# Gates spread by DMA, forgetting attention set up inside the input projection, and a delta rule on unscaled keys

## The chip, the cores and the metric

The kernel runs on one core of one Trainium2 chip. The metric is the time of one execution on the device, in microseconds (us). The engines of a core are TensorE (PE in the profile; PEld is its weight load), VectorE (DVE), ScalarE (ACT), GpSimd (POOL) and SyncE (SP), beside 16 DMA engines. Each runs its own list of instructions and waits for others on semaphores.

## The reference, cut to what matters

256 tokens of 1024 channels go through two blocks. The first has two layers, each a mixer (pooling, then attention with 16 heads) and a squared-ReLU MLP; the outcome of each of these four parts is multiplied by a gate of one value per channel before it is added to `x`. The second block puts 16 learned tokens in front, projects with `w_in` (3592 columns), and runs a gated delta rule (4 heads of 128) beside a forgetting attention (8 heads of 64):

```python
def l2norm(x): ...                       # x * rsqrt(sum(x*x) + eps)
q, k, v = split(silu(causal_dwconv(qkv, conv_w)))      # q, k, v of 4 heads x 128
q = l2norm(q) * DK ** -0.5;  k = l2norm(k);  beta = sigmoid(b_raw)
g = -exp(a_log) * softplus(a_raw + dt_bias)            # gc is its running sum
# a_mat: (k beta) k^T, below the diagonal, times exp(gc_i - gc_j)
rhs = jnp.concatenate([v * beta[..., None], k * (beta * jnp.exp(gc))[..., None]], axis=-1)
sol = lax.linalg.triangular_solve(a_mat + jnp.eye(chunk), rhs, left_side=True, lower=True, unit_diagonal=True)
u, w = sol[..., :dv], sol[..., dv:]
qk = jnp.einsum("bhncd,bhnsd->bhncs", q, k) * decay
...
v_new = u_c - w_c @ state
o_c = (q_c * exp(g_c)) @ state + qk_c @ v_new
state = state * exp(g_last) + (k_c * exp(g_last - g_c))^T @ v_new
o = o * lax.rsqrt(jnp.mean(o * o, axis=-1, keepdims=True) + EPS) * norm_w * silu(z)

# forgetting attention: c = cumsum(log_sigmoid(f_raw + f_bias))
sc = einsum("bqhd,bkhd->bhqk", q, k) * scale + c_q - c_k      # causal, softmax, times v
```

Then come `w_out`, a SwiGLU network and a last norm.

## The kernel before

Tokens are held in two tiles of 128 (index `m`), the learned tokens in one of 16 beside them (`META`). Every fp32 weight is split into a high part (`wh`, ACT, L570) and a low part (`wl`, DVE, L1074); activations are split too (`H` L1055, `L` L1057), and TensorE makes three passes for a product, H·wh, H·wl and L·wh. Weights come in tiles of 2 MB, in a ring of four slots. A tile has two halves (`hb`); a half is split in two steps, and TensorE waits for both.

Nothing is scheduled by a tool. Each engine's list is written by hand, and an engine runs its list in that order, so an instruction that waits holds up all behind it.

**Gates.** The gate vector lies with one channel to a partition (`modc`), and the residual needs it as a row on all partitions. `gate_diag` (DVE, L1018) multiplies the identity by a gate column, eight times; `gate_mm` (PE, L1668) multiplies a matrix of ones by each of these; `gate_copy` (DVE, L1026) takes the two banks to the tile `gate`. This happens for MLP0 in its last tile of `w_down`, and for the output projection `w_o` and MLP1 one after the other between attention and `w_o` (PE loop `wo_out`, L1637), behind the transposes of L1608.

**Input projection.** `w_in` has seven tiles (L1945, 272 token columns to a matmul; tile 3 is token-major, L1637). Tiles 0 to 2 give q, k, v of the delta rule, which DVE convolves (L1321), tile 3 its gate z, tiles 4 to 6 those of the forgetting attention. Small products of `wsm` give beta, the decays and the forget gate; DVE and ACT make `beta`, `gdec` and `tks` of them (L1347 to L1356, L741 to L746). ACT copies the results from PSUM (L764).

**Forgetting attention.** After the last tile PE makes the running sums (L1957, L1961), ACT copies them to `ncT` and `EG` (L771, L773), PE spreads a row of the sums to all partitions for each head (L1969), DVE copies these to `cm0`/`cm1` (L1361), and POOL masks them (L486, L489). Scores (L1978, L1981), a minimum on DVE, exponentials on ACT (L789), transposes (L2006, L2008) and the product with v (L2016 to L2020) follow in a loop over the heads, two at a time.

**Delta rule.** After the loop PE transposes q, k and v to token-major (L2027), ACT and DVE take the norms (L810, L1409), DVE scales keys and queries in eight passes and two small ones (L1427 to L1431), PE transposes all of these back (L2046, L2052), copies go to SBUF (L1434, L832), and PE makes the products K·K and Q·K (L2065, L2062). DVE multiplies them by the decays (L1448), POOL masks level 0 (L532), and the inverse of the triangular system starts: transposes (L2073, L2075), then six levels of x (L2085) and z (L2095, L2096). POOL makes each level's mask and, in between, the right sides (L513 to L520). At the end stand u, w, the state and the output with its norm (L2106 to L2134, L1493 to L1499), and the transposes for `w_out` (L1608).

## Time and profile before

| | us |
|---|---|
| median of 3 executions | 1131.53 |
| lowest, highest | 1131.45, 1134.54 |
| the profiled execution | 1124.33 |
| its span, first to last instruction | 1122.6 |
| first matmul of `w_in` | 660.98 |
| the loop over the heads, its first transpose (L2006) | 769.73 |
| first z product of level 1 | 828.36 |
| first matmul of `w_out` | 889.51 |

The profiled execution took 7.2 us less than the median; all sums are made in its times. A row of the timeline gives start, duration, engine, line, operation, output and inputs with sizes, how many instructions it groups, and in brackets the idle time before it with what ended it. A product of fp32 numbers of 128 columns counts as two instructions there, a transpose as one. The clock of a stretch is the share of full speed that was granted to TensorE: 1.00 is 2.4 GHz, 0.50 is 1.2 GHz.

### The profile page before, as it was taken

Reading aid. Unit: us, or ns where it says so; the run is one execution under the profiler, and the core shown is the slowest. Engines: PE = TensorE matmul, PEld = TensorE weight load, DVE = VectorE, ACT = ScalarE, POOL = GpSimd, SP = SyncE. Lnnn points to the kernel's source line nnn. Section 1 sums busy time; section 2 is a strip of 40 time slices with the busy share of each in tenths; the row PEclk is TensorE's granted clock in tenths of the full one; section 3 lists DMA queues with packets and bytes.
Section 4 is the critical chain, followed back from the end, with each engine's and each line's share of the span. In section 5 each row is a group of like instructions: output and inputs, shape, how many; then the busy total and the mean of one; then the engine's idle time right before and its main releaser. Section 6 shows DMA issues by size and latency. Waiting matters only on the chain.

```text
span 1122.6 us, 16534 instructions
## 1 busy us (share of the span) xinstructions
PE 1012.2 (90%) x6589; PEld 894.4 (80%) x6589; DVE 637.1 (57%) x1003; ACT 461.2 (41%) x747; POOL 112.6 (10%) x106
## 2 busy tenths in 40 slices
PE   3779999998998788899999969999789789999996
PEld 1449889996996687799889869996688669999995
DVE  1466677777546975554554465624544554454454
ACT  2344444442434212544444454536321344344343
POOL 2012010121000000111111200002063000000000
PEclk8889999999899659899999979998699789999999
DMA  9997686785546662345454523550000124646620
GB/s 327 371 387 276 231 293 226 273 288 216 198 157 220 224 226 79 144 151 215 158 215 181 213 86 105 214 168 1 1 1 1 38 75 141 196 154 204 201 78 38
DMA packets 105186, 195.60 MB, mean 174 GB/s; under 512 B 2283, under 2 KB 46572, under 8 KB 105132
## 3 DMA queue, kind: packets, MB, share of 16 engines
q1 hardware_dynamic: 104380, 192.58, 48.7%
q0 software_dynamic: 752, 2.26, 0.6%
q8 instruction: 38, 0.62, 0.2%
q14 instruction: 16, 0.13, 0.0%
HBM read 193.76 MB, written 1.07 MB: 174 GB/s over the span
## 4 chain that ended last, share of the span: by engine, by line
PE 78%; DVE 12%; ACT 3%; DMA 3%; issue 2%; POOL 1%; SPq 0%; DVEq 0%; POOLq 0%; ACTq 0%
PE ps L1691 28%; PE ps L1709 15%; PE ps L1945 7%; PE ps L2154 5%; PE ps L1637 4%; PE ps L1832 4%; DMA raw<-in_w_mod 3%; DVE wl L1074 3%; DVE accu L977 2%; ACT arena L587 1%; PE ps L2085 1%; PE ps L2096 1%; POOL x L450 1%; PE ps L1859 1%; PE ps L2095 1%
## 5 line engine op out<-in xcount | busy, mean ns | idle before, releaser
L1074 DVE TENSOR_TENSOR wl<-raw,wh 128x1024 fp32r<-128x1024 f32 (+1 forms) x288 | 315.4, 1138 | 266.9 <-ACT wh L570 266.9
L570 ACT ACTIVATE wh<-raw 128x1024 fp32r<-128x1024 f32 (+1 forms) x288 | 268.4, 982 | 352.7 <-PE ps L1691 188.3
L1691 PE MATMUL ps<-H,wh 128*128 128x256 f32 x864 | 245.4, 284 | 5.8 <-DVE L L1057 4.7
L1691 PE MATMUL ps<-H,wl 128*128 128x256 f32 x864 | 245.6, 284 | 0.0
L1691 PE MATMUL ps<-L,wh 128*128 128x256 f32 x864 | 245.2, 284 | 0.0
L1691 PEld LDWEIGHTS ps<-H,wh 128*128 128x128 f32 x864 | 166.1, 192 | 9.3 <-issue 8.3
L1691 PEld LDWEIGHTS ps<-L,wh 128*128 128x128 f32 x864 | 166.3, 192 | 0.0
L1691 PEld LDWEIGHTS ps<-H,wl 128*128 128x128 f32 x864 | 165.4, 191 | 0.9
L1709 PE MATMUL ps<-wh,aTh 128*128 128x512 f32 x256 | 101.8, 398 | 1.6 <-DVE wl L1074 1.6
L1709 PE MATMUL ps<-wl,aTh 128*128 128x512 f32 x256 | 101.2, 395 | 0.0
L1709 PE MATMUL ps<-wh,aTl 128*128 128x512 f32 x256 | 101.1, 395 | 0.0
L461 POOL TENSOR_TENSOR arena<-arena 128x512 f32<-128x512 f32 x32 | 56.2, 1755 | 309.3 <-ACT arena L615 309.3
L1945 PE MATMUL ps<-H,wh 128*128 128x272 f32 x192 | 57.8, 301 | 2.0 <-DVE L L1057 1.7
L1709 PEld LDWEIGHTS ps<-wh,aTh 128*128 128x128 f32 x256 | 48.0, 188 | 12.6 <-issue 1.6
L1945 PE MATMUL ps<-L,wh 128*128 128x272 f32 x192 | 57.4, 299 | 0.0
L1709 PEld LDWEIGHTS ps<-wh,aTl 128*128 128x128 f32 x256 | 48.0, 187 | 11.8
L1945 PE MATMUL ps<-H,wl 128*128 128x272 f32 x192 | 57.3, 298 | 0.0
L1709 PEld LDWEIGHTS ps<-wl,aTh 128*128 128x128 f32 x256 | 48.0, 188 | 11.0
L1608 PE MATMUL ps<-ident,arena 128*128 128x128 f32 x128 | 22.1, 335 | 24.2 <-DVE arena L1040 19.3
L1608 PEld LDWEIGHTS ps<-ident,arena 128*128 128x128 f32 x128 | 18.7, 175 | 27.9 <-DVE arena L1040 19.6
L1945 PEld LDWEIGHTS ps<-H,wh 128*128 128x128 f32 x192 | 38.1, 198 | 2.5 <-issue 2.5
L1832 PE MATMUL ps<-H,wh 128*128 128x256 f32 x128 | 36.8, 287 | 2.1 <-DVE L L1057 2.1
(376 smaller groups left out, 1685.3 us busy)
## 6 DMA issues: line engine op xcount, KB each, us to landing
raw<-in_w_up SPq DMA_DIRECT2D x16, 2048.0 KB, 8.7
raw<-in_w_down SPq DMA_DIRECT2D x16, 2048.0 KB, 7.7
raw<-in_w_mod SPq DMA_DIRECT2D x12, 2048.0 KB, 16.1
raw<-in_w_in SPq DMA_DIRECT2D x7, 2048.0 KB, 7.6
raw<-in_w_mod SPq DMA_DIRECT2D x12, 1024.0 KB, 7.1
raw<-in_w_qkv SPq DMA_DIRECT2D x6, 2048.0 KB, 11.1
raw<-in_w_mod SPq DMA_DIRECT2D x8, 1536.0 KB, 6.9
raw<-in_w_gate SPq DMA_DIRECT2D x11, 1024.0 KB, 5.2
```

Source lines behind the costliest of these rows:

```text
L450: e.tensor_tensor(x[:, 0, 512 * c:512 * c + 512], x[:, 0, 512 * c:512 * c + 512], tok[:, 0, 512 * c:512 * c + 512], ALU.add).then_inc(S["r ...
L461: e.tensor_tensor(act[:, 2 * b:2 * b + 2, :], r, r, ALU.mult).then_inc(S["a_done"], 1)
L570: e.activation(dst, src, ACT.Copy).then_inc(S["split_h"], 1)
L977: ins = e.scalar_tensor_tensor(out=accu[:, u, :], in0=w[:, k, :], scalar=ccol[:, 0, k:k + 1], in1=accu[:, u, :], op0=ALU.mult, op1=ALU.add)
L1074: e.tensor_tensor(o, src, i1.bitcast(F32), ALU.subtract).then_inc(S["split_l"], 1)
L1608: ins = e.transpose(ps[:, 4 + k // 2, (k % 2) * SEQ + P * m:(k % 2) * SEQ + P * m + P], tok[:, m, P * k:P * k + P], ident[:, :])
L1637: ins = e.matmul(ps[:, bank, :], src[xa][:, 4 * hb + k, META + P * m:META + P * m + P], w[wb][:, k, :], start=(hb == 0 and k == 0 and n == 0),
L1691: ins = e.matmul(ps[:, 4 + b, SEQ * c:SEQ * c + SEQ], w[wb][:, k, P * c:P * c + P], (H, L)[xa][:, k, META:TT], start=(k == 0 and n == 0), ...
L1709: ins = e.matmul(ps[:, 2 * m + c, :], (aTh, aTl)[xa][buf][:, 2 * hb + k, P * m:P * m + P], w[wb][:, k, 512 * c:512 * c + 512], start=False ...
L1832: ins = e.matmul(ps[:, b + hb, SEQ * c:SEQ * c + SEQ], w[wb][:, k, P * c:P * c + P], (H, L)[xa][:, k, META:TT], start=(k == 0 and n == 0), ...
L1945: ins = e.matmul(ps[:, b + 2 * hb + c, 0:TT], w[wb][:, k, P * c:P * c + P], (H, L)[xa][:, k, :], start=(k == 0 and n == 0), stop=(k == KD ...
L2154: ins = e.matmul(ps[:, 2 * m + c, :], (aTh, aTl)[xa][buf][:, hb, P * m:P * m + P], (wh, wl)[wb][:, hb, 512 * c:512 * c + 512], start=False ...
```

## The change

Three things are changed.

1. The gates of the MLP0, `w_o` and MLP1 residuals are no longer made by DVE and PE. POOL stores the eight columns of `modc` to a row in DRAM (1024 values of 4 bytes) and loads it back to all partitions (512 KB). The residual waits for that load.
2. The running sums stand inside tile 4 of the projection, the spreading of the forget rows in tiles 4 and 5, the sums of the decays (L2034 before) behind the first half of tile 6. For that DVE makes the decays ahead of the split of tile 4 and not behind it. ACT does SiLU of q and k in tile 5 and the rest in tile 6.
3. Keys and queries are not scaled. K·K and Q·K are made from the feature-major `yT` before the attention loop; squared norms of keys are the diagonal of K·K (POOL multiplies by the identity, DVE sums). The factor beta/norm² is multiplied into both matrices, the first inverse is made inside the loop, and the right sides take the norms that are left. The norm of the queries goes into the output norm: their squares are summed by PE after level 6 (`q_mm`), and DVE adds the term to the mean square (`out_bias`). Transposes of k and v (`token_major`) fill the places of t0 and level 1.

POOL, the gates:

```diff
+            def gate_store(i, l, col, ready):
+                e.wait_ge(S["mod_col"], ready)
+                e.dma_start(gate_rows[i].rearrange("(r p) -> p r", p=P), modc[:, l, col:col + 8],
+                            allow_slow_non_contiguous=True).then_inc(S["gate_out"], 16)
+            def gate_load(i, dst):
+                e.wait_ge(S["gate_out"], 16 * (i + 1))
+                e.dma_start(gate[dst][:, :], gate_rows[i].partition_broadcast(P)).then_inc(S["gate_in"], 16)
+            squares(1)
+            squares(2)
+            gate_store(0, 0, 40, 12)
+            squares(3)
+            gate_load(0, 1)
...
             residual()
+            gate_store(1, 1, 16, 18)
+            gate_load(1, 0)
+            gate_store(2, 1, 40, 19)
+            gate_load(2, 1)
```

POOL, in the second block:

```diff
+            e.wait_ge(S["tk_d"], 8)
+            e.wait_ge(S["split_used"], 2 * T_WIN + 2)
+            for m in range(NM):
+                e.tensor_tensor(DL[:, m, :, :], masks[:, 7, :].unsqueeze(1).broadcast_to([P, GH, P]),
+                                bc(gdec[:, 1 + m, :], P, P), ALU.mult).then_inc(S["dl_p"], 1)
...
+            for m in range(NM):
+                e.wait_ge(S["at_d"], 2 + m)
+                e.tensor_tensor(Al[:, m], AT[:, m], ident[:, :].unsqueeze(1).broadcast_to([P, GH, P]),
+                                ALU.mult).then_inc(S["dg_p"], 1)
+            e.wait_ge(S["f_set"], 3)
+            f = coef[:, 0]
+            for m in range(NM):
+                e.tensor_tensor(AT[:, m], AT[:, m], bc(f[:, 1 + m, :], P, P), ALU.mult).then_inc(S["at_f"], 1)
```

ACT, inside the loop over the tiles of the projection:

```diff
+                    if (i, c) == (4, 1):
+                        e.wait_ge(S["nc_mm"], 1)
+                        e.activation(ncT, ps[0:FH, 2, 0:TT], ACT.Copy, scale=float(DH) ** 0.5).then_inc(S["nc_set"], 1)
+                        e.wait_ge(S["gs_mm"], 2)
+                        e.activation(EG[:, 1:3, :], ps[:, 3, 0:24].rearrange("p (s c) -> p s c", s=2), ACT.Exp
+                                     ).then_inc(S["gs_set"], 1)
```

DVE, behind the loop over the heads and behind level 6:

```diff
-            scaled(0)
...
-            scaled(1)
...
+            e.tensor_scalar(coef[:, 3, 1:3, :], ps[:, 3, 0:8].rearrange("p (m h) -> p m h", m=NM), EPS, EPS * P,
+                            ALU.add, ALU.mult).then_inc(S["q_set"], 1)
+            def out_bias(m):
+                e.wait_ge(S["on_sq"], 5 * m + 4)
+                e.scalar_tensor_tensor(out=onrm[:, 1, m, :], in0=onrm[:, 0, m, :], scalar=1.0 / P, in1=coef[:, 3, 1 + m, :],
+                                       op0=ALU.mult, op1=ALU.add).then_inc(S["ob_set"], 1)
```

PE, inside the projection and behind level 6:

```diff
                             if c == 0:
                                 ins.then_inc(S["pj_mm"], 1)
+                                if (i, hb) == (4, 0):
+                                    gate_sums()
+                                if (i, hb) in ((4, 1), (5, 0)):
+                                    forget_rows(4 * (i - 4))
                     ins.then_inc(S["split_used"], 1)
+                    if (i, hb) in ((4, 1), (5, 0)):
+                        forget_rows(4 * (i - 4) + 2)
+                    if (i, hb) == (6, 0):
+                        e.wait_ge(S["pj_ev"], 22)
+                        decay_sums()
...
+            e.wait_ge(S["qg_p"], 2)
+            for m in range(NM):
+                for h in range(GH):
+                    ins = e.matmul(ps[:, 3, GH * m + h:GH * m + h + 1], qsq[:, m, h, :], ones[:, 0:1], start=True, stop=True)
+            ins.then_inc(S["q_mm"], 1)
```

Three places of the order are shown. First VectorE around the split of tile 4, before (each `x4` split is one tile's four quarters; `tks`, `eb` and `gdec` are the small operands of the decays):

```order
478 L1321 SCALAR_TENSOR_TENSOR arena<-arena,pcol 128x272 [waits conv] x8
479 L1074 TENSOR_TENSOR wl<-raw,wh 128x1024 [waits split_h] x4
480 L1347 TENSOR_SCALAR eb<-eb 128x12 [waits tk_a]
481 L1349 RECIPROCAL beta<-eb 128x12 [waits tk_d]
482 L1351 TENSOR_SCALAR nega<-nega 128x4 [waits tk_a]
483 L1353 SCALAR_TENSOR_TENSOR tks<-tks 128x36 [waits tk_a]
484 L1356 TENSOR_TENSOR gdec<-tks,nega 128x12 [waits tk_d]
485 L1074 TENSOR_TENSOR wl<-raw,wh 128x1024 [waits split_h] x8
486 L1361 COPY cm_55<-ps 128x272 [waits bc_mm] x8
```

and now:

```order
471 L1341 SCALAR_TENSOR_TENSOR arena<-arena,pcol 128x272 [waits conv] x8
472 L1347 TENSOR_SCALAR eb<-eb 128x12 [waits tk_a]
473 L1349 RECIPROCAL beta<-eb 128x12 [waits tk_d]
474 L1351 TENSOR_SCALAR nega<-nega 128x4 [waits tk_a]
475 L1353 SCALAR_TENSOR_TENSOR tks<-tks 128x36 [waits tk_a]
476 L1356 TENSOR_TENSOR gdec<-tks,nega 128x12 [waits tk_d]
477 L1100 TENSOR_TENSOR wl<-raw,wh 128x1024 [waits split_h] x6
478 L1363 COPY arena<-ps 128x272 [waits bc_mm] x4
479 L1100 TENSOR_TENSOR wl<-raw,wh 128x1024 [waits split_h] x2
480 L1363 COPY arena<-ps 128x272 [waits bc_mm] x4
481 L1100 TENSOR_TENSOR wl<-raw,wh 128x1024 [waits split_h] x4
```

The five small instructions, the fourth of which waits for ACT (`tk_a`), now stand ahead of the split of tile 4, and the copies of the forget rows between the quarters of tile 5.

Second, TensorE behind the first half of tile 6 and behind the last tile of `w_in`, now (L1979 the products of the learned tokens' keys, L1985 and L1989 the decay sums, L2034 key products, L2046 and L2049 the first scores, L2056 the decays spread to all partitions for the queries):

```order
2911 L1979 MATMUL ps<-arena 16x16 [waits silu_set,pj_ev]
2912 L1979 MATMUL ps<-arena 16x16 x3
2913 L1985 MATMUL ps<-wtri,arena 128x128 [waits dl_p]
2914 L1985 MATMUL ps<-wtri,arena 128x128 x3
2915 L1985 MATMUL ps<-wtri,arena 128x128 [waits dl_p]
2916 L1985 MATMUL ps<-wtri,arena 128x128 x3
2917 L1989 MATMUL ps<-wtri,arena 16x16 [waits dl_p]
2918 L1989 MATMUL ps<-wtri,arena 16x16 x3
```

and behind the last tile:

```order
2967 L2034 MATMUL ps<-arena 128x128 [waits at_d]
2968 L2034 MATMUL ps<-arena 128x128 x7
2969 L2046 MATMUL ps<-arena 128x272 [waits pj_ev]
2970 L2046 MATMUL ps<-arena 128x272
2971 L2049 MATMUL ps<-arena 128x144 x2
2972 L2056 MATMUL ps<-wtri,gdec 128x128 x8
2973 L2034 MATMUL ps<-arena 128x128 [waits silu_set,e_set]
```

The sums stood behind the last tile or behind the loop before; the key products stood behind the loop and sixteen transposes.

Third, TensorE between attention and `w_o`, before (L1608 the transposes of the attention's output, L1668 the two gates, L1637 `w_o`):

```order
1606 L1608 MATMUL ps<-ident,arena 128x128 [waits o_ev,mod_col]
1607 L1608 MATMUL ps<-ident,arena 128x128 x7
1608 L1608 MATMUL ps<-ident,arena 128x128 [waits o_ev]
1609 L1608 MATMUL ps<-ident,arena 128x128 x7
1610 L1668 MATMUL ps<-arena,ones 128x128 [waits gate_diag] x8
1611 L1668 MATMUL ps<-arena,ones 128x128 [waits gate_diag,gate_set]
1612 L1668 MATMUL ps<-arena,ones 128x128 [waits gate_diag] x7
1613 L1637 MATMUL ps<-wh,H 128x512 [waits hs_l,split_l,gate_set]
```

and now:

```order
1604 L1635 MATMUL ps<-ident,arena 128x128 [waits o_ev,mod_col]
1605 L1635 MATMUL ps<-ident,arena 128x128 x7
1606 L1635 MATMUL ps<-ident,arena 128x128 [waits o_ev]
1607 L1635 MATMUL ps<-ident,arena 128x128 x7
1608 L1664 MATMUL ps<-wh,H 128x512 [waits hs_l,split_l]
```

The sixteen gate products and their waits are gone, and `w_o` follows the transposes.

## Rows read from the trace of the kernel before

**Rows 1.** The page: the chain that ended last, shares of the span by engine.

```profile
PE 78%; DVE 12%; ACT 3%; DMA 3%; issue 2%; POOL 1%; SPq 0%; DVEq 0%; POOLq 0%; ACTq 0%
```

**Rows 2.** Stretches: window, length, PE, PEld, DVE, ACT, POOL busy (count), clock, DMA.

```profile
759.60:769.80 10.20, 9.43 (x32) 5.80 (x32) 5.29 (x16) 7.02 (x11) 6.32 (x7) 0.52 0.00 1
769.80:786.50 16.70, 16.70 (x117) 13.04 (x117) 7.74 (x31) 8.76 (x35) 1.99 (x3) 1.00 0.01 1
786.50:800.20 13.70, 12.25 (x51) 10.74 (x51) 4.96 (x9) 0.40 (x2) 0.00 (x0) 0.50 0.00 1
```

**Rows 3.** Timeline of PE and DVE in the last tile of MLP0.

```profile
261.05 1.95 PE L1668 MATMUL ps<-arena,ones 128*128 128x128 f32 x16
262.75 0.48 PE L1709 MATMUL ps<-wh,aTh 128*128 128x512 f32 x1
262.34 2.36 DVE L1074 TENSOR_TENSOR wl<-raw,wh 128x1024 fp32r<-128x1024 f32 x2 [0.54 <-ACT wh L570]
```

**Rows 4.** Timeline of PE, ACT and DVE between attention and `w_o`.

```profile
421.57 3.46 PE L1608 MATMUL ps<-ident,arena 128*128 128x128 f32 x16 [0.28 <-DVE modc L1263]
424.06 2.32 ACT L601 ACTIVATE hf<-ps 128x256 f32<-128x256 f32 x8 [12.34 <-PE ps L1608]
430.56 0.41 DVE L1055 CAST H<-hf 128x512 fp32r<-128x512 f32 x1
431.85 0.47 PE L1637 MATMUL ps<-wh,H 128*128 128x512 f32 x1 [1.93 <-DVE L L1057]
```

**Rows 5.** Timeline of ACT, DVE and POOL around the split of tile 4.

```profile
716.77 0.32 ACT L746 ACTIVATE tks<-tks,ones 128x36 f32<-128x36 f32 x1
715.01 2.35 DVE L1074 TENSOR_TENSOR wl<-raw,wh 128x1024 fp32r<-128x1024 f32 x2
721.90 0.17 DVE L1356 TENSOR_TENSOR gdec<-tks,nega 128x12 f32<-128x12 f32 x1
769.51 2.04 POOL L502 TENSOR_TENSOR DL<-gate,gdec 128x512 f32<-128x512 f32 x2
```

**Rows 6.** Timeline of DVE, and of POOL with its squares, in MLP0.

```profile
158.23 3.20 DVE L1074 TENSOR_TENSOR wl<-raw,wh 128x1024 fp32r<-128x1024 f32 x2
...
152.43 1.70 POOL L461 TENSOR_TENSOR arena<-arena 128x512 f32<-128x512 f32 x1 [19.03 <-ACT arena L615]
158.08 1.13 POOL L461 TENSOR_TENSOR arena<-arena 128x512 f32<-128x512 f32 x1 [3.95 <-ACT arena L615]
```

**Rows 7.** The chain that ended last, behind `w_in`: start, us, what.

```profile
717.51 36.57 PE ps L1945 x288
754.55 1.63 PE ps L1957 x6
756.18 1.43 PE ps L1961 x12
...
758.93 5.59 PE ps L1969 x12
764.52 1.21 PE ps L1978 x4
...
794.26 1.30 DVE arena L1389 x2
...
862.10 0.70 DVE arena L1466
```

**Rows 8.** Timeline of PE from the key products to level 1.

```profile
818.35 2.02 PE L2065 MATMUL ps<-arena 128*128 128x128 f32 x16 [0.78 <-ACT arena L832]
826.01 2.12 PE L2085 MATMUL ps<-arena,Al 128*128 128x128 f32 x16
828.36 0.49 PE L2095 MATMUL ps<-X,arena 128*128 128x128 f32 x2
```

**Rows 9.** The page, DMA issues: what, how many, KB each, us to landing.

```profile
gate<-in_norm_final SPq DMA_DIRECT2D x1, 512.0 KB, 9.0
wsm<-in_w_in POOLq DMA_DIRECT2D x2, 32.0 KB, 6.7
```

More of the change, by code:

```diff
@@ new lines, in right_sides @@
+                    e.wait_ge(S["eg_set"], 2)
+                    for m in range(NM):
+                        e.tensor_tensor(QgT[:, m], yT[:, 0:GH, META + P * m:META + P * m + P], EGb[:, m], ALU.mult
+                                        ).then_inc(S["qg_p"], 1)
+            for lv in range(1, 7):
+                for g in groups(lv):
+                    if lv > 1:
+                        e.wait_ge(S["x_mm"], count(lv - 1, g) + 1)
+                    else:
+                        e.wait_ge(S["t0_set"], g + 1)
+                    level_mask(lv, g)
@@ L782, in _ @@
+            for m in range(NM):
+                e.wait_ge(S["eg_mm"], m + 1)
+                e.activation(EGb[:, m], ps[:, 6 + m, :].rearrange("p (h c) -> p h c", h=GH), ACT.Exp).then_inc(S["eg_set"], 1)
             for h in range(FH + 1):
@@ L1924, in small_projections, with gate_sums @@
                 ins.then_inc(S["sm_mm"], 1)
+            tri = wtri[:, META + P:META + 2 * P]
+            def gate_sums():
+                e.wait_ge(S["tk_d"], 8)
+                e.wait_ge(S["made2"], 9)
+                for s, (v0, w) in enumerate(((META + P, META), (P, P), (0, P))):
+                    ins = e.matmul(ps[0:FH, 2, 0:TT], tks[0:w, 1, s, 4:12], wtri[0:w, v0:v0 + TT], start=(s == 0), stop=(s == 2))
+                ins.then_inc(S["nc_mm"], 1)
+                for s in range(NM):
+                    for c, lhs in enumerate((tri, masks[:, 7, :], ones[:, :])):
+                        ins = e.matmul(ps[:, 3, 12 * s + 4 * c:12 * s + 4 * c + 4], lhs, gdec[:, 1 + s, :], start=True, stop=True)
+                ins.then_inc(S["gs_mm"], 1)
+                e.matmul(ps[0:META, 3, 32:36], masks[0:META, 7, 0:META], gdec[0:META, 0, :], start=True, stop=True
+                         ).then_inc(S["gs_mm"], 1)
@@ new lines, in forget_rows, with tok_cols @@
+            def forget_rows(h0):
+                e.wait_ge(S["nc_set"], 1)
+                e.wait_ge(S["gs_set"], 2)
+                for h in (h0, h0 + 1):
+                    if h >= 2:
+                        e.wait_ge(S["cm_raw"], h - 1)
+                    e.matmul(ps[:, 2 + h % 2, 0:TT], ident[0:FH, h:h + 1].broadcast_to([FH, P]), ncT, start=True, stop=True
+                             ).then_inc(S["bc_mm"], 1)
+            def tok_cols(blk, m):
+                return yT[:, blk, META + P * m:META + P * m + P]
```

499 lines of the change are left out of this document (227 added, 272 removed).

## The prediction

> **What bounds the kernel now.** I read the last chain by engine first [rows 1]: 78% of the span is TensorE, 12% VectorE, 3% ScalarE. So an edit is worth what it takes from TensorE's list, or from a wait in it, and VectorE is the next to look at. Then I took the chain behind the input projection [rows 7]: the last three tiles run without a gap, 288 matmuls in 36.57 us or 0.127 each, and behind them stands a row of small steps, up to z of level 1 at 828.36 [rows 8]. The stretches [rows 2] show the third thing: TensorE's granted clock. It is 0.52 from 759.6 to 769.8, 1.00 to 786.5, then 0.50 to 800.2. Work in this region runs at either of two levels, 1.2 and 2.4 GHz, and a wait in it can cost more than its own length.
>
> All times below are in the times of the profiled execution of before, 1124.33 us; it lies 7.2 under the median of 1131.53.
>
> **MLP0's gate.** TensorE is rid of 1.70 (261.05 to 262.75, [rows 3]). But the split of the weight half it needs next starts at 262.34 and takes 2.36, so it ends at 264.70. TensorE has half of this half-tile's work before it needs the second quarter, and would want that at about 263.85 when it comes 1.70 earlier. So it waits 0.85, and the gain is 0.85; between 0.8 and 1.7, since VectorE also loses eight multiplications there. **−0.8.**
>
> The gate's load is issued by POOL behind its third pair of squares, at 158.08 + 1.13 = 159.2 [rows 6]. The nearest row is another load of 512 KB to all partitions, which lands after 9.0 us [rows 9]; this one is wanted more than 100 us later, so it hides behind MLP0. Its bytes run beside a weight tile under way, and are a quarter of such a tile's. I take 0, since TensorE is seldom short of a tile there, between 0 and an estimated +1.
>
> **The two gates between attention and w_o.** Before, TensorE starts sixteen transposes at 421.57 and `w_o` at 431.85; between lie both gates [rows 4]. Now only ACT's copy of the first half (424.06, eight pieces in 2.32, two of which are wanted: 424.64), VectorE's cast 0.41 and the rest of its split up to the release (430.56 to 431.85 is 1.29 for both) stand behind the transposes: 424.64 + 1.29 = 425.93, say 426.0. **−5.85.** Nothing hides this, since the split of the weights was done long before. The loads are issued at 421.3 at the latest, behind two stores, and are wanted at about 440, by 9.0 + 6.7 us [rows 9] at 437.
>
> **From tile 4 to level 1.** Here the change removes, adds and moves. I rebuild TensorE's list from 717.51 on.
>
> *Tile 4 starts later.* Its weights' low parts were split at 715.01 for 2.35 us a half [rows 5]. Now VectorE first makes the decays, and these wait for ACT's last logarithm, which ends at 716.77 + 0.32 = 717.09. Two small instructions of some 0.2 follow [rows 5], to 717.54; the split's 2.35 ends at 719.9, and tile 4 starts at 720.1, +2.6. At the same moment POOL is released to make DL (2.04 for two, [rows 5]), beside the split. A split beside a POOL square took 3.20 and not 2.35 [rows 6], so I add 0.85: 720.95, **+3.4**.
> The Trainium skill, *SBUF — State Buffer*, *Who interferes with whom*, says that a VectorE instruction with two SBUF inputs contends with a GpSimd instruction that reads SBUF, and that the one issued first blocks the other altogether. The square of [rows 6] lasted 1.13, and 0.85 was lost, which is nearly that. By that rule the split would lose all of DL's 2.04, and tile 4 would start at 722.1, +1.2 on my sum.
>
> *Sums inside the projection.* Gate sums 1.63 + 1.43 = 3.1 [rows 7]; then the forget rows wait for ACT, which has a weight half and two copies ahead of `ncT` and the table of Exp, all of which DVE's and PE's lists leave waiting: 1.4, an estimate from two copies at 0.4 and the small ones (0 to 3). Eight forget rows: 5.59 for six at half clock [rows 7, 2], so 0.466 each at full clock, 3.6; a wait of 0.5 for VectorE's last copies. Decay sums: eight products of 128 columns at 2.02/8 [rows 8] and eight small ones, 2.75. With these the projection ends not at 754.1 but at 754.1 + 3.4 + 3.1 + 1.4 + 3.6 + 0.5 + 2.75 = 768.85.
>
> *The clock.* Tile 4's wait and the earlier tail of tile 3 make nearly 4 us without a matmul. I take +1.0 for a stretch at half clock behind it (0 to 5.1, which is what the stretch of 10.20 at 0.52 loses at most, [rows 2]). Which of the two it will be no row tells.
> The Trainium skill, *TensorE: Matmul & The Clock Gate*, *What's actually happening*, says that the throttled state is the default and activity releases it; by it a longer wait at tile 4 costs twice, once as a wait and once as slow matmuls.
>
> *To the loop.* Key products 2.0 (eight, [rows 8]), the first scores 0.9 (1.21 and a half at half clock), the decays spread for the queries 2.05, query products 2.05, twelve transposes of v 1.75, 0.7 for the copies that the loop needs: 769.85 + 9.45 = 779.3. Before it was 769.73: the loop starts 9.5 later, since all of this was behind it.
>
> *The loop* took 769.73 to 794.2. It keeps its instructions on TensorE; VectorE gets `key_factors` and the first inverse, about 1.15 of which I count as visible. Where the clock falls in it may change; I keep the same share at half clock (some 7.6 of 24.4 us, [rows 2]). It ends at 804.8.
>
> *Behind the loop.* Gone: 32 transposes, the norms, eight scalings, sixteen transposes and more back, the products at 818.35 [rows 8]. Left: t0 2.0, twelve transposes 1.5, and 0.9 for copies that queue behind VectorE's two output copies (1.30, [rows 7]); x of level 1, 2.35 (826.01 to 828.36); twelve transposes 1.5; a wait of 2.0 for ACT, which has four copies ahead of X (0 to 2.4). Sum 10.25, so z of level 1 is at 815.05, where it was at 828.36. **−13.4.** POOL must have level 0 and the right sides ready: its list of masks, factors and z's weights, summed at 1.02 to 1.25 a piece (DL's and the mask's), ends about 5 us before level 1 wants it and 1.3 us before level 2 does.
>
> **Behind the levels.** Query sums: sixteen records at 1.43/12 [rows 7] are 1.9, plus 0.4 for VectorE's step with which TensorE must wait, less the 0.70 in which it waited for the last update anyway [rows 7]: **+1.6**. The output norm: `out_bias`, 0.17 like other tiny steps [rows 5], and two hand-overs on the path to the last transposes, **+0.75** (0.4 to 1.5).
>
> **Sum:** −0.8 − 5.85 − 13.4 + 1.6 + 0.75 = −17.7. The profiled execution would be 1106.6, the median 1131.53 − 17.7 = 1113.8; I say **1114**.
>
> **The rivals.**
>
> *A. The cover is thinner than it looks.* The projection was TensorE's best stretch, and the change puts five places into it where it waits for ACT, VectorE or POOL. If the wait for ACT is 3 (+1.6), the clock costs 5.1 (+4.1) and the loop 2 more, −17.7 becomes −10.0 and the time 1121.5. For it: ACT and VectorE have no slack at tile 4 [rows 5]. Against it: the 288 matmuls have no gap today [rows 7], so the tiles behind are ready in time.
>
> *B. The clock stays up.* If the loop and the steps behind it run at full clock, 13.7 us at 0.50 [rows 2] hold some 5 us to be had, since TensorE now has no long wait behind the loop. Then −23, the time 1108.5. Against it: within the loop nothing is shorter.
>
> *C. Slower than before.* The store writes 1024 pieces of 4 bytes. The nearest row is a load of 32 KB in 1024 pieces of 32 bytes, which lands after 6.7 us [rows 9]. If the store took far longer, POOL, which waits for it ahead of its fourth square, would hold the squares and with them MLP0's `w_down`. The store is issued where the wait before 152.43 began, 152.43 − 19.03 = 133.4 [rows 6], so even the load's place, 159.2, is 25.8 us behind. Past that POOL is late, and each us more is a us for the squares, at most. So the store must take 25.8 + 17.7 + 3.4, or 47 us, seven times the row, before the kernel is slower by what counts: 1135 at that point, and 1 more for each us more. The two later stores stand one behind the other with some 12 us to spare; each would have to take 16 us to eat the gain.
>
> *D. POOL takes VectorE's place.* The gates' gain is there, but the levels wait for POOL, which now makes diagonals, factors, the query mask and z's weights one after the other. Its pieces take 1.02 (DL, [rows 5]) or 1.70 (a square, [rows 6]). Twelve pieces lie between the factors and level 1's masks, so at 1.70 they end 12 × 0.68 = 8.2 later, and with the two right sides behind them and the slack of 5 and 1.3 that I count, the levels start some 6 late: −11.7, 1119.8.
>
> **How the numbers follow.** My own forecast 0.5 (1110 to 1118), A 0.17, B 0.17, D 0.12, C 0.03, something not thought of 0.01. The range takes in A, B and D: 1106 to 1122. A measurement of this kernel can tell 0.3%, or 3.4 us, from no change; so faster takes a time under 1128.1. Faster 0.92 (all but C, and a little of A and D), same 0.04, slower 0.04.
>
> **What would show it.** In the changed kernel: `w_o`'s first matmul about 6 us after the start of the sixteen transposes and no gate products; the first z of level 1 at 154 us behind the first matmul of `w_in` (before 167.4), less what comes earlier; tile 4 beginning some 3.4 us late behind a split that started after ACT's logarithm; POOL's DL beside it; no scaling of keys. It would be wrong if tile 4's wait were under 1 us or over 5, if the loop grew by more than 2 us, if x of levels 1 or 2 waited for `Al` from POOL, or if a weight tile came late beside a gate's load.

## The result

| | us |
|---|---|
| before, median of 4 executions beside the change | 1131.88 (1131.45 to 1134.54) |
| the change, median of 4 | 1119.47 (1116.11 to 1122.24) |
| ratio, 95% interval | 0.9886 (0.9870 to 0.9902) |
| forecast | 1114 (1106 to 1122) |
| profiled execution of the change, its span | 1119.65, 1117.9 |

The kernel got 12.4 us faster; the forecast was 17.7. The time is in the range, 5.5 us over the forecast. Of the changed kernel's profile, the chain that ended last answers to [rows 1], and the DMA of the gates to [rows 9].

```profile
PE 79%; DVE 11%; ACT 4%; issue 2%; DMA 2%; POOL 1%; SPq 0%; DVEq 0%; ACTq 0%; POOLq 0%
...
gate<-gate_rows POOLq DMA_DIRECT2D x3, 512.0 KB, 6.0
gate_rows<-modc POOLq DMA_DIRECT2D x3, 4.0 KB, 11.3
```

TensorE still makes the chain. A store of 1024 pieces of 4 bytes lands after 11.3 us, where the nearest row of before gave 6.7 [rows 9]; the load takes 6.0, where it gave 9.0.

The profiled execution of before, 1124.33, is one of its quick ones, for of the 52 executions of the kernel before in the groups of runs below, seven took 1124.0 to 1127.0 and the others 1130.9 to 1135.1. So the kernel before was profiled once more (below, 1133.32). The table has the length of each stage from TensorE's timelines, in us, from the first matmul of one stage to that of the next. "Quick" is the profile that the prediction rests on. The stretch ahead of MLP0's first large matmul is not in it: that took 81.5 to 85.8 in the fourteen profiles of this study, whatever the edit, so two profiles can differ by 4 us for no reason of the edit.

| stage | before, quick | before, again | the change | forecast: change less quick | measured: change less again |
|---|---|---|---|---|---|
| MLP0 | 202.69 | 203.47 | 200.78 | −0.8 | −2.7 |
| attention's end to w_o | 10.28 | 10.99 | 4.58 | −5.85 | −6.4 |
| w_o to MLP1 | 32.73 | 34.11 | 34.28 | 0 | +0.2 |
| w_in to tile 4 | 56.53 | 56.21 | 59.47 | +3.4 | +3.3 |
| tile 4 to the projection's end | 36.55 | 36.56 | 52.83 | +12.35 (clock 1.0 in it) | +16.3 |
| to the loop over the heads | 15.67 | 15.87 | 8.63 | −6.2 | −7.2 |
| the loop | 24.42 | 27.69 | 32.88 | +1.15 | +5.2 |
| to z of level 1 | 34.21 | 33.91 | 9.76 | −24 | −24.2 |
| levels 1 to 6 | 34.48 | 34.49 | 35.62 | +1.6 | +1.1 |
| u, w, state, output norm | 26.67 | 26.68 | 28.83 | +0.75 | +2.2 |

The large step is as forecast: 24 us of transposes, scalings and norms behind the loop are gone. Ahead of the loop 16 came back inside the projection, and 7 went between the projection and the loop. What is off is what TensorE's clock did. In these stretches of the changed kernel (columns as in [rows 2]) it is low behind the wait at tile 4, and again through most of the loop:

```profile
716.46:721.20 4.74, 4.74 (x25) 4.59 (x26) 3.06 (x2) 0.00 (x0) 1.98 (x2) 0.64 0.09 10
...
730.60:738.80 8.20, 6.94 (x34) 5.92 (x33) 2.00 (x4) 2.40 (x6) 0.00 (x0) 0.79 0.01 2
738.80:769.10 30.30, 29.68 (x233) 28.10 (x233) 10.37 (x13) 15.52 (x22) 7.19 (x5) 1.00 0.43 140
777.90:784.60 6.70, 6.17 (x43) 4.79 (x43) 5.15 (x20) 3.83 (x15) 2.25 (x4) 1.00 0.00 0
784.60:810.80 26.20, 26.20 (x104) 20.36 (x103) 7.88 (x25) 7.28 (x23) 11.60 (x13) 0.51 0.00 1
```

Before, in the quick profile, the loop ran at 1.00 up to 786.5 [rows 2], that is for 17 of its 24 us. Now it has 6.7 us at full clock and 26.2 at half.

Tile 4 in the changed kernel, timeline of PE, DVE and POOL (answers to [rows 5]):

```profile
716.46 0.36 PE L2014 MATMUL ps<-H,wh 128*128 128x272 f32 x1 [3.62 <-DVE wl L1100]
713.03 0.17 DVE L1356 TENSOR_TENSOR gdec<-tks,nega 128x12 f32<-128x12 f32 x1
713.12 6.41 DVE L1100 TENSOR_TENSOR wl<-raw,wh 128x1024 fp32r<-128x1024 f32 x4
713.34 3.88 POOL L498 TENSOR_TENSOR arena<-gate,gdec 128x512 f32<-128x512 f32 x2 [63.64 <-DVE gdec L1356]
717.18 1.26 POOL L500 TENSOR_TENSOR arena<-gate,gdec 16x64 f32<-16x64 f32 x1
```

The wait is 3.62 where it was 0.34. VectorE's split and POOL's products stand side by side, and both are slow: POOL's two take 3.88 and not 2.04 [rows 5], the small one 1.26 and not 0.28.

### The profile page after: what moved, and what is told of

It reads as the page before. It is cut to its first block, busy times and chain, and to the rows that moved or that the text cites. A ratio compares the mean times of both kernels' runs of the same rounds, so it can differ in the third digit from the quotient of the medians.

```text
span 1117.9 us, 16342 instructions
## 1 busy us (share of the span) xinstructions
PE 1016.2 (91%) x6525; PEld 896.8 (80%) x6525; DVE 618.8 (55%) x954; ACT 454.1 (41%) x726; POOL 132.3 (12%) x124
## 3 DMA queue, kind: packets, MB, share of 16 engines
HBM read 195.33 MB, written 1.09 MB: 176 GB/s over the span
## 4 chain that ended last, share of the span: by engine, by line
PE 79%; DVE 11%; ACT 4%; issue 2%; DMA 2%; POOL 1%; SPq 0%; DVEq 0%; ACTq 0%; POOLq 0%
PE ps L1718 28%; PE ps L1736 15%; PE ps L2014 7%; PE ps L2208 5%; PE ps L1664 5%; PE ps L1857 4%; DVE wl L1100 3%; DVE accu L1003 2%; DMA raw<-in_w_mod 2%; ACT arena L623 1%; PE ps L2126 1%; PE ps L1635 1%; PE ps L2143 1%; POOL x L441 1%; PE ps L2142 1%
## 5 line engine op out<-in xcount | busy, mean ns | idle before, releaser
L1100 DVE TENSOR_TENSOR wl<-raw,wh 128x1024 fp32r<-128x1024 f32 (+1 forms) x288 | 319.0, 1150 | 269.9 <-ACT wh L606 269.8
L1718 PE MATMUL ps<-H,wh 128*128 128x256 f32 x864 | 245.2, 284 | 5.6 <-DVE L L1083 4.6
L1718 PEld LDWEIGHTS ps<-H,wl 128*128 128x128 f32 x864 | 165.3, 191 | 0.9
L1635 PE MATMUL ps<-ident,arena 128*128 128x128 f32 x128 | 24.7, 363 | 24.7 <-DVE arena L1066 19.3
L2014 PEld LDWEIGHTS ps<-H,wl 128*128 128x128 f32 x192 | 39.5, 206 | 0.0
```

The source lines that it names most:

```text
L1100: e.tensor_tensor(o, src, i1.bitcast(F32), ALU.subtract).then_inc(S["split_l"], 1)
L1635: ins = e.transpose(ps[:, 4 + k // 2, (k % 2) * SEQ + P * m:(k % 2) * SEQ + P * m + P], tok[:, m, P * k:P * k + P], ident[:, :])
L1718: ins = e.matmul(ps[:, 4 + b, SEQ * c:SEQ * c + SEQ], w[wb][:, k, P * c:P * c + P], (H, L)[xa][:, k, META:TT], start=(k == 0 and n == 0), ...
L2014: ins = e.matmul(ps[:, b + 2 * hb + c, 0:TT], w[wb][:, k, P * c:P * c + P], (H, L)[xa][:, k, :], start=(k == 0 and n == 0), stop=(k == KD ...
```

## The experiments

**The kernel before, again.** No edit.

> The kernel before, unchanged, once more. In the first pair of profiles the change looks like 4.7 us (1124.33 to 1119.65), in the medians like 12.4 (1131.88 to 1119.47). If the profiled execution of before was an unusually quick one, this trace is near 1131 us and shows where the other 7 us lie; I expect them in the loop over the heads, as a stretch at half clock (it ran at full clock from 769.8 to 786.5). If instead the profile adds nothing and takes nothing, it is near 1124 again.

1132.93 median, ratio to before 0.9998 (0.9977 to 1.0019); profiled execution 1133.32. The extra time of this profile over the quick one lies in small pieces: 3.6 us ahead of the first large matmul, 0.8 in MLP0, 0.7 at attention's end, 1.4 in w_o, and 3.3 in the loop. So the loop is one place of it, not the only one. Its clock changed between the two levels several times in the loop, where [rows 2] had 1.00 for the first 16.7 us:

```profile
778.00:790.00 12.00, 12.00 (x67) 9.26 (x67) 4.37 (x18) 5.12 (x20) 0.00 (x0) 0.80 0.01 2
```

All comparisons of stages below are with both profiles of before.

**The gates alone.** The kernel before with the first part of the change.

```diff
-            gate_diag(modc[:, 1, 16:24])
-            gate_copy(0)
-            gate_diag(modc[:, 1, 40:48])
-            gate_copy(1)
...
-            gate_mm()
-            e.wait_ge(S["gate_set"], 6)
-            gate_mm()
-            e.wait_ge(S["gate_set"], 8)
```

> Before, with the first part of the change alone: the gates of MLP0, w_o and MLP1 by DMA. My theory from the two traces: 1.8 us at MLP0 and 5.5 between attention and w_o, less 1.8 given back because w_o's first matmuls then run at half clock; together 5 to 6 us faster than before (ratio 0.995). The rival, my sum of the prediction, says 6.65. If the load of 512 KB disturbed the weights, it would be under 4.

1125.20 against 1132.55, ratio 0.9932 (0.9910 to 0.9954): 7.3 us. MLP0 took 200.83. Over all profiles of this study it takes 202.45 to 203.47 with the old gate (four, mean 203.0) and 200.68 to 202.53 with the new one (ten, mean 201.5), so the gate is worth some 1.5 there. The stretch to w_o went from 10.28 and 10.99 to 4.58. w_o itself took 34.27, as in the second profile of before (34.11). Against the quick profile the low clock at its head gives back 1.5, against the second one 0.2. Over the fourteen profiles w_o took 32.7 to 32.8 in seven, 34.1 to 34.3 in six and 35.0 in one, and the groups don't follow the edits. The timeline of TensorE shows the place and the slow matmuls (0.63 at half clock; the first row of w_o answers to the last of [rows 4]):

```profile
422.03 3.67 PE L1621 MATMUL ps<-ident,arena 128*128 128x128 f32 x16 [0.28 <-DVE modc L1280]
426.61 0.77 PE L1650 MATMUL ps<-wh,H 128*128 128x512 f32 x1 [0.91 <-DVE L L1076]
427.18 0.63 PE L1650 MATMUL ps<-wl,H 128*128 128x512 f32 x1
```

**The rest alone.** The changed kernel with the old gates, that is the second and third parts.

```diff
-            gate_load(2, 1)
...
+            gate_mm()
+            e.wait_ge(S["gate_set"], 6)
+            gate_mm()
+            e.wait_ge(S["gate_set"], 8)
```

> The changed kernel with the gates of MLP0, w_o and MLP1 made again by VectorE and TensorE: its second and third parts alone. The gates alone brought 7.3 us (1132.55 to 1125.20). If the parts add, this one is 5 us faster than before (1127). Theory: they add within 1.5 us, since they are hundreds of microseconds apart. Rival: the projection's sums and the unscaled keys bring next to nothing by themselves, because the loop at half clock eats them (within 2 us of before), and the rest came from the gates' place.

1117.71 against 1131.74, ratio 0.9881 (0.9864 to 0.9897): 14.0 us. So the parts don't add: 7.3 and 14.0 give 21.3, and the whole change has 12.4. Neither theory said that. The stages tell where: tile 4 at 59.52 and the projection at 52.80 are as in the changed kernel, the loop took 24.84 and not 32.88, and the output norm's stage 25.61 and not 28.83. The instructions of the loop are the same in both. These are rows of the same place in it, two records of a product of 64 columns behind the scores of heads 4 and 5, first here and then in the changed kernel:

```profile
794.74 0.43 PE L2086 MATMUL ps<-vtm,arena 16*128 16x64 f32 x2
```

```profile
787.23 0.69 PE L2092 MATMUL ps<-vtm,arena 16*128 16x64 f32 x2
```

**The decays behind the first half of the split.**

```diff
                 if i == 4:
+                    split(T_WIN + i, landed(N_WIN + i)[0], cols=True, qs=(0, 1))
                     gate_decays()
-                if i == 5:
+                    split(T_WIN + i, landed(N_WIN + i)[0], cols=True, qs=(2, 3))
+                elif i == 5:
```

> The changed kernel, with VectorE's decays between the two halves of the split of tile 4 and not ahead of it. Theory: tile 4 then starts some 3 us sooner, since its first half is split at 710.8 and not at 713.1, and DL on POOL meets the split of the second half, which has slack; the kernel gets 3 us faster than the change, 4 to 6 if the stretch at half clock behind the wait goes too. Rival: the gate sums then wait for the decays by as much, and nothing moves (within 1 us).

1111.78 (1106.19 to 1118.02) against 1132.55, ratio 0.9833 (0.9773 to 0.9893); the changed kernel had 0.9886, and the two intervals overlap, so the stages have to decide. Tile 4 starts 56.03 behind the projection's start and not 59.47, and the stage behind takes 49.76 and not 52.83: the wait cost 3.4 and slow matmuls behind it 3.1, together 6.5, where I had expected 4 to 6. TensorE's timeline, and VectorE's with POOL beside it, now with the second half:

```profile
714.34 0.36 PE L2016 MATMUL ps<-H,wh 128*128 128x272 f32 x1 [0.34 <-DVE wl L1100]
715.89 3.21 DVE L1100 TENSOR_TENSOR wl<-raw,wh 128x1024 fp32r<-128x1024 f32 x2 [1.03 <-ACT wh L606]
715.00 3.02 POOL L498 TENSOR_TENSOR arena<-gate,gdec 128x512 f32<-128x512 f32 x2 [63.97 <-DVE gdec L1356]
```

The meeting with POOL is still there (3.21 and 3.02), but TensorE doesn't wait for it. The executions took 1106.19 and 1107.38, 1116.17 and 1118.02; the profile is of 1107.38, in which the loop took 28.26 and the output norm's stage 27.20, so it doesn't show where the other two lost 9 to 11.

**DL held back.** POOL's three products wait for the whole split.

```diff
             e.wait_ge(S["tk_d"], 8)
+            e.wait_ge(S["split_l"], 4 * (T_WIN + 5))
```

> The changed kernel, with POOL's DL held back until VectorE has split all of tile 4. In the changed kernel the three decay products of POOL ran beside that split and took 3.88 and 1.26 us instead of 2.04 and 0.28, and three quarters of the split took 5.18. Theory: without the meeting the first half of the split takes 2.35 again and tile 4 starts 0.9 to 1 us sooner (59.5 us behind the first matmul of the projection becomes 58.5); the rest of the wait stays, since it is the decays' place. In the time that is 1 us plus what the clock makes of it. Rival: the contention was all of the wait, and tile 4 starts 3 us sooner as in the run with the decays behind the first half.

Tile 4 starts 58.70 behind the projection's start, 0.8 sooner than in the changed kernel. So of the 3.3 us of delay 0.8 are contention and 2.5 the place of the decays. But the stage behind took 54.28 at a mean clock of 0.91, 1.5 more than in the changed kernel, and the output norm's stage 31.65 at 0.66, 2.8 more: with a shorter wait the clock took more back. VectorE and POOL, apart:

```profile
718.18 0.36 PE L2015 MATMUL ps<-H,wh 128*128 128x272 f32 x1 [2.77 <-DVE wl L1101]
715.68 4.63 DVE L1101 TENSOR_TENSOR wl<-raw,wh 128x1024 fp32r<-128x1024 f32 x4
720.54 2.04 POOL L499 TENSOR_TENSOR arena<-gate,gdec 128x512 f32<-128x512 f32 x2 [68.34 <-DVE wl L1101]
722.53 0.28 POOL L501 TENSOR_TENSOR arena<-gate,gdec 16x64 f32<-16x64 f32 x1
```

Four pieces of the split take 4.63 alone and 6.41 beside POOL. The median, 1118.80 (1112.77 to 1125.71, ratio 0.9859, 0.9806 to 0.9911), can't tell 1 us: its executions spread over 13.

**Twelve products more in the loop.** Two for each of six heads, into columns that are written later.

```diff
                 if h % 2 == 0 and 2 <= h < FH:
                     fox_scores(h)
+                for r in range(2 if 2 <= h < 8 else 0):
+                    e.matmul(ps[:, r, 384:512], ident[:, :], tri, start=True, stop=True)
```

> The changed kernel, with twelve fp32 products of 128 columns more in the loop over the heads (two for each of six heads, into columns that are written later). They are pure extra work: 12 x 0.25 = 3 us at full clock. Theory: the loop got 8.4 us longer than before because TensorE's granted clock fell at 784.6, in its third pair of heads, and stayed at 0.50 to 815; if more work keeps the clock up, the loop gets shorter by 5 to 10 us in spite of the extra work. Rival: the clock does not answer to this, and the loop gets 3 to 6 us longer.

1106.40 (1104.33 to 1115.40) against 1132.55, ratio 0.9798 (0.9745 to 0.9850): 26.2 us faster than before, about 14 more than the change, for work that does nothing. The loop took 24.10 us with its extra work, 8.8 less than in the changed kernel, and the output norm's stage 25.62, 3.2 less, though nothing was edited there. One of the four executions took 1115.40. The whole loop is at full clock (columns as in [rows 2]):

```profile
775.98:800.08 24.10, 24.10 (x170) 19.74 (x171) 12.99 (x45) 11.11 (x38) 13.86 (x15) 1.00 0.01 2
```

**Six of them.** The same with `range(1 if 2 <= h < 8 else 0)`.

> The changed kernel with six products more in the loop, one for each of six heads, half of those in the earlier run. Theory: the clock answers to how busy TensorE is, so six are either as good (loop about 23 us, 1.5 less work) or do little (loop 28 to 33 us); between them the loop's length tells how near the edge it is. If the earlier gain came from something else than the clock, for instance from PSUM banks or the order of waits, six should bring about half of the 8.8 us.

1105.41 (1104.33 to 1106.90), ratio 0.9763 (0.9743 to 0.9782); loop 24.21. Six are as good as twelve, so half the work doesn't bring half the gain. In the third and fourth pair of heads, where the changed kernel was at half, the clock is full; it falls only behind them, some 4 us ahead of the loop's end:

```profile
784.00:792.00 8.00, 8.00 (x57) 6.39 (x55) 4.06 (x18) 4.48 (x18) 7.00 (x8) 1.00 0.00 1
792.00:800.00 8.00, 8.00 (x46) 6.65 (x46) 3.35 (x6) 2.78 (x6) 3.15 (x3) 0.79 0.00 1
```

**The same twelve in the kernel before.**

> The kernel before, with the same twelve products more in its loop over the heads. Its loop took 24.4 us in one profile and 27.7 in another, at full clock for a part. Theory: the clock falls in any version of this loop, and a denser TensorE keeps it up; the loop takes 23 to 25 us with the extra work, the kernel 2 to 4 us less than before. Rival: only the changed kernel's loop is short of work (it has more small waits for VectorE and POOL), and the kernel before gets up to 3 us slower by the extra work.

1124.89 (1123.72 to 1126.90), ratio 0.9930 (0.9909 to 0.9952); loop 24.46. The loop's mean clock was 0.98, where it was 0.84 and 0.73 in the two profiles of before. So the loop of before has the weakness too, and 3 us of extra work cost it nothing. The median fell by 7.5, more than I expected and more than the loop shows: it took 27.69 in the second profile of before and 30.36 in the kernel with the gates alone, 3 to 6 us over this one. The rest isn't explained by an edit in the loop; w_o (32.74, not 34.11) and MLP0 (202.45, not 203.47) stand 2.4 lower here than in the second profile of before.

**Both edits.** The decays between the halves, and the twelve products.

> The changed kernel with both edits: the decays between the halves of tile 4's split, and the twelve products in the loop. Theory: the two act at different places, one 6.5 us ahead of the loop's start (3.4 of wait and 3 of slow matmuls), the other inside it, so they add: 13 + 6 us faster than the changed kernel, about 1100. Rival: the earlier run with the decays moved had gained part of its time in the loop too (28.3 against 32.9), so together they bring only 13 + 3, about 1103.

1100.26 (1099.07 to 1100.30), ratio 0.9710 (0.9692 to 0.9727): 32.1 us under before, as the first theory said. Tile 4 at 56.01, the projection 49.75, the loop 24.45. The four executions lie within 1.3 us of each other.

**Without the queries' norm.** Both edits, less the sums of squares, VectorE's step and `out_bias`.

```diff
-            e.wait_ge(S["qg_p"], 2)
-            for m in range(NM):
-                for h in range(GH):
-                    ins = e.matmul(ps[:, 3, GH * m + h:GH * m + h + 1], qsq[:, m, h, :], ones[:, 0:1], start=True, stop=True)
-            ins.then_inc(S["q_mm"], 1)
-            e.wait_ge(S["q_set"], 1)
```

> The version with both edits, less the norm of the queries in the output norm: no sums of their squares on TensorE, no step of VectorE behind them, no out_bias; the output norm takes a constant instead. It leaves out that part of the computation. My prediction priced it at 1.6 behind the levels and 0.75 in the output norm. The traces say 1.13 (35.63 against 34.49 for the levels) and 0.5 (idle before the last transposes 5.19 against 4.69). Theory: 1.6 us faster than the version with both edits, by those two stages. Rival: 2.35 us, my prediction; or nothing, if the clock behind is what sets the stage.

The levels take 34.52 and not 35.63, the output norm's stage 25.04 and not 25.61: 1.1 and 0.6, together 1.7. The medians say 1.9 (1098.37). TensorE's wait ahead of the last transposes, with both edits and here:

```profile
863.86 1.97 PE L1637 MATMUL ps<-ident,arena 128*128 128x128 f32 x8 [5.19 <-DVE arena L1528]
```

```profile
860.25 1.97 PE L1624 MATMUL ps<-ident,arena 128*128 128x128 f32 x8 [4.70 <-DVE arena L1515]
```

**Products in the last wait.** Both edits, and eighteen products between the transposes of the two token tiles ahead of w_out.

```diff
                         if m == 1 and k % 2:
                             ins.then_inc(S["tr_done"], 1)
+                    for r in range(fill if m == 0 else 0):
+                        e.matmul(ps[:, 2 + r % 2, 0:P], ident[:, :], wtri[:, 0:P], start=True, stop=True)
```

> The version with both edits, with eighteen fp32 products of 128 columns more between the transposes of the first and of the second token tile ahead of w_out, where TensorE waits 5.19 us for the output norm. At 0.25 they take 4.5 us, inside the wait. Theory: the clock stays up, so the eight transposes take 1.0 and not 1.97, and the first eleven matmuls of w_out 0.23 and not 0.43: 3 us faster. Rival: the clock falls by something else, or the extra products delay the transposes: 0 to 1 us slower.

1097.63 (1096.74 to 1098.48), ratio 0.9695 (0.9679 to 0.9711), 2.6 faster than with both edits and the fastest of all; the products compute nothing. The transposes take 1.09 where they took 1.97. In the profile the output norm's stage is 0.24 shorter, and `w_out`, from its first matmul to the first of the SwiGLU network, takes 30.29 and not 32.32:

```profile
857.79 4.18 PE L1642 MATMUL ps<-wtri,ident 128*128 128x128 f32 x36
863.14 1.09 PE L1637 MATMUL ps<-ident,arena 128*128 128x128 f32 x8 [1.17 <-DVE arena L1528]
```

**The changed kernel, later.** Sixteen products ahead of w_o.

```diff
             feature_major([(S["o_ev"], 4)] * 2)
+            for r in range(16):
+                e.matmul(ps[:, 2 + r % 2, 0:P], ident[:, :], wtri[:, 0:P], start=True, stop=True)
```

> The changed kernel with sixteen fp32 products of 128 columns more ahead of w_o, some 350 us before the loop over the heads. They do nothing for the result and make all that follows start later, by 4 us at full clock and 8 at half, less about 1 of idle time. From the projection on the instructions are the changed kernel's, word for word. With the old gates in that place (two parts of the change alone) the loop took 24.84 us and ran at full clock; in the changed kernel it took 32.88. Theory: the moment at which the loop comes decides, not its code, so a shift by 3 to 7 us moves the loop's time somewhere between 24 and 33 us and the whole kernel does not get slower by the shift; if the loop lands on 24.8, the kernel is 2 to 5 us faster in spite of the added work. Rival: the loop of the changed kernel is at 33 us for a reason of its own (the gates' DMA, another wait), stays there, and the kernel is 3 to 7 us slower.

1118.02 (1114.75 to 1120.07), ratio 0.9892 (0.9857 to 0.9926). The kernel got neither slower nor clearly faster (1119.47 before this edit, and the intervals overlap). The products took 3.74 us, but only 2.15 more stood between the attention's end and w_o (6.73, not 4.58), and w_o, with its clock up from the start, took 32.76 and not 34.28. That the products did this is not shown, since w_o took 32.72 to 32.76 in four kernels with the new gates and without these products. Other stages moved as well, so that the projection began at 657.70, 0.7 later than in the changed kernel, and its loop took 32.49. The shift that I wanted did not come about, so this run doesn't decide between its two theories. It shows only that sixteen products in that place cost the kernel nothing that its medians can tell.

## Why the prediction was right, and where it was off

**The number is better than its parts.** From the projection's first matmul to z of level 1 I forecast −13.4 (the prediction's own times give −13.3). It measures 170.24 us in the second profile of before and 163.57 in the changed kernel, that is −6.7, and −3.8 against the quick profile. Half of the main gain did not come. The kernel is still only 5.5 off, for MLP0 came out 1.9 better than forecast (0.7 by the means) and attention's end 0.55, and the stretch ahead of MLP0 happened to be 1.5 shorter than in the second profile of before. That part is luck. I had also put a sum made in the quick profile's times on a median 7.2 above it. And one sign that I had named for being wrong did appear: the loop grew by more than 2 us.

**What held.** The bound (TensorE), the direction, and what left the region behind the loop (24.2 measured, 24 forecast). What came back ahead of it was under-priced, as the next parts show. The place of the gates after attention: forecast −5.85, measured −5.7 and −6.4 by the two profiles of before. Tile 4's delay: forecast +3.4 with 0.85 for POOL beside the split; measured +3.3, and 0.8 of it contention. The Trainium skill, *SBUF — State Buffer*, *Who interferes with whom*, would have had the split lose all of DL's 2.04; the start of tile 4 lost 0.8, and the four pieces together 1.78, while POOL's products took 1.84 and 0.98 longer. So both engines lost time there, not the one that came second alone. The two pieces of work are 4.63 and 2.32 apart, 6.95 in sum, and 6.41 side by side, so they went nearly one after the other, with the loss shared. For the start of tile 4 my 0.85 was the right price, and the 2.04 that I took from the Trainium skill's rule too high.

**MLP0's gate, −0.8.** This reading was wrong. I read the split at 262.34 [rows 3] as that of the half whose matmuls start at 262.75. But those matmuls use their low part at once, so it was split long before, and the split at 262.34 is for the half after it. Nothing makes TensorE wait, and the 1.70 can be gained whole; the means above say 1.5. In the changed kernel the same split stands at 264.31, the next half begins at 269.43, and TensorE has no wait in between:

```profile
264.31 2.36 DVE L1100 TENSOR_TENSOR wl<-raw,wh 128x1024 fp32r<-128x1024 f32 x2 [0.34 <-ACT wh L606]
...
269.43 0.48 PE L1736 MATMUL ps<-wh,aTh 128*128 128x512 f32 x1
```

**The sums inside the projection, 11.35 with 1.4 for ACT.** The wait for ACT came out at 1.26. The gate sums were right in size too (3.1), and so was the wait for VectorE's copies (0.62, not 0.5). With the decays moved, where the clock stays at 1.00 in it, the stage takes 49.76, 13.2 more than before; my 11.35 was 1.9 short. I gave a forget row 0.466 by halving the row at half clock; a pair takes 1.11 to 1.15 at full clock, so eight take 4.5 and not 3.6. The other 1.0 is spread over the pauses between matmuls and sums; I did not pin it down.

**The clock behind tile 4, +1.0 (0 to 5.1).** A term that was mis-sized: 3.1, by the run with the decays moved. The first 4.74 us of tile 4 run at 0.64 and the 8.20 around its forget rows at 0.79, seen above, with 1.00 between them; each is 1.7 lost. The second of these stretches starts behind the wait of 1.26 for ACT, 14 us later, and is gone too when tile 4 starts in time. The Trainium skill, *TensorE: Matmul & The Clock Gate*, *What's actually happening*, has activity release the throttle; by it the wait is paid twice, and this place agrees: 3.4 as a wait and 3.1 behind it. The second price doesn't follow from the wait's length, though: with DL held back the wait was 2.77, and the stage took 54.28, 4.5 more than at full clock.

**The loop, "the same share at half clock".** This step failed, and it is the largest miss: +1.15 forecast, +5.2 measured against the second profile of before (+8.5 against the quick one). The stage ahead, with +12.35 forecast and +16.3 measured, is the other large one (1.9 for the sums, 2.1 for the clock). I took the quick profile's clock for the loop's property. It isn't: without extra products the loop took 24.42, 27.69 and 30.36 us in kernels with the old loop, and 24.84, 28.26, 32.49, 32.88 and 33.27 with the new one. With extra products it took 24.10 to 24.46 in six profiles, five with the new loop and one with the old. The 24.10 of the run with twelve products are all at full clock and hold 3 us of extra work. Without that work the loop at full clock would take some 20 to 21 us, by my estimate from its lengths and mean clocks: 24.42 × 0.84, 27.69 × 0.73, 24.84 × 0.85 and 32.88 × 0.61 are 20.5, 20.2, 21.1 and 20.1. `key_factors` and the first inverse, for which I gave 1.15, show as one wait of 0.51 in the new loop, where the quick profile has none:

```profile
782.99 0.43 PE L2092 MATMUL ps<-vtm,arena 16*128 16x64 f32 x2 [0.51 <-DVE arena L1443]
```

The clock, and not a new wait, makes all the rest. That is shown. What makes the clock fall is not. No long gap does: in the quick profile TensorE was busy for all of the 16.70 us ahead of the fall at 786.5 [rows 2], and in the changed kernel its last gap ahead of the fall at 784.6 is the 0.51 above. What is different from the dense tiles ahead is that many products are small (64 or 16 rows or columns). That it is this, I argue from the fact that six larger products change it; the runs don't separate that from other ways in which they act.

**What set the loop apart between kernels with the same loop** stays open. What differs is when in the loop the clock falls: some 7 us into it in the changed kernel, 17 us into it in the same kernel with the old gates. The old gates, 350 us ahead, gave 24.84; the new ones 32.88 and, with products ahead of w_o, 32.49. The moment at which the loop comes was my theory, and the run for it moved the loop's start by 1.0 us only (778.92, not 777.92). In the five profiles of the new loop without extra products it starts at 772.74, 777.92, 778.92, 781.10 and 786.39 and takes 28.26, 32.88, 32.49, 33.27 and 24.84, so no order shows. Each changed kernel has one profile, and the kernel before, unchanged, took 24.42 in one and 27.69 in the other, so part of these differences can be that of one execution from the next.

**The queries' norm: +1.6 and +0.75.** Measured 1.1 and 0.6. In the changed kernel the output norm's stage took 2.2 more, but in five other profiles with the same instructions there it took 25.61 or 25.62, which is 1.1 less than before, and in two more 27.20 and 31.65. The stage's mean clock was 0.89 or 0.90 in the five, 0.83 and 0.66 in the two, and 0.81 in the changed kernel: the difference is the clock again.

**The rivals.** A had its 3 us of slow matmuls and its loop, but for another reason than waits: there is only 0.51 more of waiting in the loop than before. B's mechanism (the clock) was the right one, with the sign of the other side. D did not come: TensorE doesn't wait for POOL in the levels. What the list of waits has for it there (engine, tile and line, what it waited for; us, times, longest) is one wait for ACT, which I had at 2.0:

```profile
PE ps L2142 <- ACT X L870: 1.3, 1, 1.3
PE ps L2126 <- issue: 1.1, 2, 0.5
```

C didn't come either: the store needed 11.3 of its 25.8 us.

## What to carry to other kernels

Ask of an engine's idle 3 us not only what it costs but at which clock the work behind it runs; here a delay of 3.4 cost 6.5, and one of 2.7 in another run 7.2. Profile the kernel before more than once ahead of pricing a change by it, above all where a stretch is at full clock in one execution: a sum may start from a quick execution without knowing it. Where TensorE runs many small products and its clock is low by the profile, try a few larger ones that do nothing. They are cheap to add, and six of them brought this kernel some 14 us, 8.7 of them in the loop itself; the kernel before, with twelve, got 7.5.

## What the runs showed of the hardware that I had not expected

TensorE's granted clock fell from 1.00 to 0.50 behind 16.70 us in which TensorE had no idle time by the profile [rows 2], with many small products; in the changed kernel it fell so with no gap longer than 0.51 in the 6.7 us ahead. With six fp32 products of 128 columns (0.25 us each) more in the changed kernel's loop it stayed at 1.00 for 20 of 24 us, and all four executions lie within 2.6 us; with twelve, 19 of 20 executions of five kernels lie within 4 us of their kernel's quickest, and one, 1115.40 beside 1104.33, does not.

The kernel's times go with the clock: its mean over the whole execution is 0.916 to 0.920 for the seven executions of before that took 1124.0 to 1127.0, and 0.907 to 0.915 for the other 45.

A store of 1024 pieces of 4 bytes landed after 11.3 us (median of three), 1.7 times as long as a load of 1024 pieces of 32 bytes (6.7).
